# A hybrid decoder block: the second half's first norm moved from VectorE to ScalarE and GpSimd

## The reference

```python
def rmsnorm(x, g):
    xf = x.astype(jnp.float32)
    y = xf * lax.rsqrt(jnp.mean(xf * xf, axis=-1, keepdims=True) + EPS)
    return (y * g.astype(jnp.float32)).astype(x.dtype)
...
        h = rmsnorm(x, norm_mix[l])
        proj = jnp.einsum('bsd,de->bse', h, w_in[l])
        x_lru = proj[..., :D_LRU]
        g_lru = proj[..., D_LRU:2 * D_LRU]
        v_cm = proj[..., 2 * D_LRU:2 * D_LRU + D_CM]
        g_cm = proj[..., 2 * D_LRU + D_CM:]
        glu = v_cm * jax.nn.sigmoid(g_cm)
        d = causal_depthwise_conv(glu, dw31_w[l], dw31_b[l])
```

## Time and profile before

| | before |
|---|---|
| median of 3 runs (lowest, highest) | 2034.61 us (2033.06, 2035.32) |
| the profiled execution | 2033.8 us, span 2032.0 us |
| PE busy | 1945.1 us, 96% of the span |
| DVE busy | 1158.7 us, 57% |
| ACT busy | 785.1 us, 39% |
| POOL busy | 1064.7 us, 52% |

### The profile page before, as it was taken

How to read it: one execution, slowest core, us unless ns; L and a number is a source line. 1 busy time by engine, 2 the same in 40 slices (tenths; PEclk the granted TensorE clock), 3 DMA queues, 4 the chain that set the end, 5 groups by cost and what they waited for, 6 DMA issues and landing times.

```text
span 2032.0 us, 23427 instructions
## 1 busy us (share of the span) xinstructions
PE 1945.1 (96%) x8602; PEld 1601.1 (79%) x8602; DVE 1158.7 (57%) x1205; ACT 785.1 (39%) x896; POOL 1064.7 (52%) x384
## 2 busy tenths in 40 slices
PE   6999899978999799999999899999999999999998
PEld 5888687856887588888888688888888888888886
DVE  5899899988545544543344534334333544574546
ACT  6356756584544433333333433233232111321112
POOL 2477477864543557765555555555555335335431
PEclk9999999978999899999999999999999999999999
DMA  5223232244768323532325332232247322242312
GB/s 162 63 63 101 66 94 76 97 150 171 249 201 259 104 88 114 154 125 76 105 67 160 125 103 67 78 103 67 78 144 290 114 83 94 91 186 89 117 41 83
DMA packets 213392, 238.60 MB, mean 117 GB/s; under 512 B 9902, under 2 KB 165550, under 8 KB 210010
## 3 DMA queue, kind: packets, MB, share of 16 engines
q1 hardware_dynamic: 213338, 237.89, 35.6%
HBM read 172.84 MB, written 65.01 MB: 117 GB/s over the span
## 4 chain that ended last, share of the span: by engine, by line
PE 84%; DVE 5%; POOL 4%; issue 2%; DMA 2%; ACT 2%; SPq 1%; DVEq 0%; POOLq 0%; ACTq 0%
PE ps L1738 20%; PE ps L1739 20%; PE ps L1740 20%; PE acc L1738 8%; PE acc L1739 7%; PE acc L1740 7%; DVE acc L1554 1%; DMA y_raw<-d_scr 1%; DVE x L1716 1%; DVE x L1707 1%; PE ps L1763 1%; DVE wo_lo L1491 1%; DVE a_lo L1569 1%; POOL w_lo L690 1%; POOL a_lo L807 0%
## 5 line engine op out<-in xcount | busy, mean ns | idle before, releaser
L1554 DVE SCALAR_TENSOR_TENSOR acc<-glu,par,acc 128x1024 f32<-128x1024 f32 x232 | 299.0, 1289 | 7.2
L802 POOL TENSOR_TENSOR t_lo<-t_sum,t_hi 128x2048 fp32r<-128x2048 f32 x44 | 204.3, 4643 | 179.3 <-ACT t_hi L1194 179.3
L796 POOL TENSOR_TENSOR b_lo<-m_raw,b_hi 128x1536 fp32r<-128x1536 f32 x44 | 158.4, 3599 | 209.4 <-ACT b_hi L1189 209.4
L1593 DVE TENSOR_TENSOR t_sum<-m_raw 128x512 f32<-128x512 f32 x88 | 134.6, 1532 | 207.7 <-PE acc L1740 110.0
L1707 DVE TENSOR_TENSOR x<-x,ps 128x512 f32<-128x512 f32 x264 | 179.5, 688 | 108.5 <-PE ps L1740 108.5
L872 POOL TENSOR_TENSOR f_lo<-f_raw,f_hi 128x2048 fp32r<-128x2048 f32 x22 | 102.5, 4659 | 260.1 <-ACT f_hi L1332 260.1
L1738 PE MATMUL ps<-h_hi,w_hi 128*128 128x512 f32 x512 | 202.0, 395 | 5.1 <-POOL w_lo L690 2.6
L1738 PE MATMUL ps<-wd_hi,f_hi 128*128 128x512 f32 x528 | 205.5, 389 | 0.2 <-DVE x L1707 0.2
L1739 PE MATMUL ps<-wd_lo,f_hi 128*128 128x512 f32 x528 | 205.4, 389 | 0.0
L1740 PE MATMUL ps<-wd_hi,f_lo 128*128 128x512 f32 x528 | 205.4, 389 | 0.0
L1739 PE MATMUL ps<-h_lo,w_hi 128*128 128x512 f32 x512 | 199.9, 390 | 0.0
(11 more groups left out here) (208 smaller groups left out, 4539.7 us busy)
## 6 DMA issues: line engine op xcount, KB each, us to landing
m_raw<-in_w_gate SPq DMA_DIRECT2D x88, 256.0 KB, 4.1
m_raw<-in_w_up SPq DMA_DIRECT2D x88, 256.0 KB, 3.8
f_scr<-gt SPq DMA_DIRECT2D x88, 256.0 KB, 2.4
f_raw<-f_scr SPq DMA_DIRECT2D x22, 1024.0 KB, 4.8
wd_raw<-in_w_down SPq DMA_DIRECT2D x22, 1024.0 KB, 4.9
w_raw<-in_w_in SPq DMA_DIRECT2D x32, 512.0 KB, 5.3
xt<-in_x SPq DMA_DIRECT2D x16, 512.0 KB, 4.1
row<-in_x SPq DMA_DIRECT2D x16, 512.0 KB, 4.9
```

The lines of the kernel that those rows point to most:

```text
L796: g.tensor_tensor(b_lo[b][:, :, :, :], m_raw[b][:, 0:3], f32(b_hi[b][:, :, :, :]), ALU.subtract).then_inc(s_mlo, 1)
L802: g.tensor_tensor(t_lo[b][:, :, :, :], t_sum[b][:, :, :, :], f32(t_hi[b][:, :, :, :]), ALU.subtract).then_inc(s_mlo, 1)
L1554: ins = v.scalar_tensor_tensor(out=into[:, :], in0=t[:, k:k + HALF], scalar=col(j, R_DW + k), in1=acc[:, :], op0=ALU.mult, op1=ALU.add)
L1593: v.tensor_tensor(into, in0, in1, ALU.subtract).then_inc(s_t, 1)
```

## The change

In the first half nothing changes. For tiles 8 to 15, `x_norm` is split in three: VectorE keeps the reciprocal (`x_reciprocal`, each one tap earlier than `x_norm` was), ScalarE multiplies the tile by it (`x_scale`), and GpSimd multiplies by the weight row (`x_gain`). Each step waits for the one before it, over two new semaphores.

```diff
         X_NORM_AT = (7, 8, 9, 10, 12, 13, 14, 15)
+        X_NORM_BETWEEN = 5
+        X_NORM_AT = (6, 7, 8, 9, 11, 12, 13, 14)
         X_LO_AT = (9, 10, 11, 12, 14, 15, 16, 17)
...
+            def x_gain(g):
+
+                pool.wait_ge(s_xsc, g - TPH + 1)
+                t = xt[g % 3]
+                nc.gpsimd.tensor_tensor(t[:, :], t[:, :], g_row[:, :], ALU.mult).then_inc(s_xn, 1)
...
                 if u >= 1:
                     gated_input(u - 1)
                     decay(u - 1)
+                    if u == NJ - 1:
+                        for n in range(X_NORM_BETWEEN):
+                            x_gain(TPH + n)
                     decay_square(u - 1)
+                if u == NJ - 1:
+                    x_gain(TPH + X_NORM_BETWEEN)
                 short_sums(u)
+                if u == NJ - 1:
+                    for n in range(X_NORM_BETWEEN + 1, TPH):
+                        x_gain(TPH + n)
...
+            def x_scale(g):
+                act.wait_ge(s_xrec, g - TPH + 1)
+                a.activation(xt[g % 3][:, :], xt[g % 3][:, :], ACT.Copy, scale=rstd[:, g:g + 1]).then_inc(s_xsc, 1)
...
                 if u == NJ - 1:
-                    for g in range(TPH, TPH + 3):
-                        x_std(g)
+                    x_std(TPH)
+                    x_std(TPH + 1)
+                    x_scale(TPH)
+                    x_std(TPH + 2)
+                    x_scale(TPH + 1)
+                    x_scale(TPH + 2)
...
                     x_std(TPH + 3)
                     x_hi(TPH + 1)
+                    x_scale(TPH + 3)
                     x_std(TPH + 4)
                     x_hi(TPH + 2)
+                    x_scale(TPH + 4)
                     x_hi(TPH + 3)
                     x_std(TPH + 5)
+                    x_scale(TPH + 5)
...
                     x_hi(TPH + 4)
                     x_std(TPH + 6)
-                if u == NJ - 1:
+                    x_scale(TPH + 6)
                     x_hi(TPH + 5)
                     x_std(TPH + 7)
+                    x_scale(TPH + 7)
                     x_hi(TPH + 6)
...
+            def x_reciprocal(g):
+                dve.wait_ge(s_std, g + 1)
+                v.reciprocal(rstd[:, g:g + 1], rstd[:, g:g + 1]).then_inc(s_xrec, 1)
+
...
                             if place == X_NORM_AT[g]:
-                                x_norm(TPH + g)
+                                x_reciprocal(TPH + g)
```

More of the change, by code:

```diff
@@ L203, in hybrid_block @@
         s_xn = sem("x_normed")
+        s_xrec = sem("x_reciprocal_ready")
+        s_xsc = sem("x_scaled")
         s_hhi = sem("h_hi_ready")
```

## The result

The changed kernel takes 2047.81 us, the median of 4 runs (2046.53 to 2048.32), against 2034.96 us (4 runs, 2033.06 to 2036.68): +12.85 us, a ratio of 1.0062 with a 95% interval of 1.0047 to 1.0077. It is slower, by the size forecast.

The account below looks back on a forecast made before the run. TensorE, busy nearly throughout, is bound by its waits. Delays through the scales, gain and inversion reach turn 15 as +12.4 us, never given back: 2032.0 + 12.4 = 2044.4 span, 2047.0 on the median's footing; range 2044.1 to 2049.1, 70 in 100.

Parts of the forecast that it names:

- Turn 8: Tile 8's transposes on TensorE wait for scale and gain: 210.2 instead of 206.97, +3.2 us, 5.3 idle before.
- Turns 9 and 10: Next transposes on TensorE: 215.7 after a low clock, then 220.6 after the later load, Sqrt and `x_lo(9)`.
- Up to `two_minus`: ScalarE's list with six added scales: `two_minus` starts at 228.9 instead of 223.07, +5.8 us.
- GpSimd: Tile 13's gain stands ahead of the first short sum, adding 1.7 us net; `x_hi(12)` moves to 238.45, +7.3.
- The reciprocal of tile 14: On VectorE it waits until 242.2 for tile 14's Sqrt, with a tap and `x_lo(12)` queued behind it.
- Turn 13: Tile 13's transposes on TensorE wait 12 us for `x_lo(12)`: 244.4 instead of 232.51, +11.9 us.
- the inversion: On VectorE, tile 14's reciprocal ahead of `x_lo(12)` waits for a Sqrt behind `x_hi(12)`; costs 4.5 us alone.
- Turns 14 and 15: Last transposes on TensorE, after tile 15's reciprocal ahead of `x_lo(13)`: 250.45 and 254.25, +12.2 us, or 255.1.
- the first of the two ways: Tile 15's transposes on TensorE at +12.2 us; the second, a low clock lasting 5.2 us, gave +13.1; +12.4 taken.
- rival 1: At tile 13's transposes, the 4.26 us wait absorbs earlier delay: +4.5 to +8, 2039 to 2043 us; 15 in 100.
- that only the inversion is left: Same as rival 1: delay up to Turn 13 absorbed, 2039 to 2043 us; 15 in 100.
- That VectorE's relief pays: Rival for VectorE's second-half passes: 1.5 us of TensorE waits vanish, 2033.1 us, no slower; 4 in 100.
- That a late stage falls apart: Rival at projection 9: `scan_input` or weight split slips, some 4 us more, 2051 us; 11 in 100.

Follow-up runs that it names:

- experiment 1: Changed kernel with the reciprocals of tiles 14 and 15 one tap later, behind `x_lo(12)` and `x_lo(13)`: 2045.1 us, ratio 1.0036.
- experiment 3: Kernel before with `x_norm(14)` put ahead of `x_lo(12)`, a tap between, no work moved between engines: 2041.11 us, ratio 1.0024.
- experiment 4: Kernel before with `x_hi(12)` and tile 14's Square and Sqrt ahead of the second evacuation, `x_hi(13)` and tile 15's behind the second product: 2033.09 us, ratio 0.9982.
- experiment 5: experiment 4 with VectorE's passes moved, `x_lo` one place earlier from tile 12 on, `x_hi(14)` ahead of the GELU table load: 2035.8 us, ratio 1.0005.
- experiment 8: Changed kernel with tile 8 alone normalised by VectorE's pass as before: 2045.1 us, ratio 1.0049.
- experiment 2: experiment 1 plus `two_minus` moved ahead of the first evacuation and `decay_square` behind the third gain: 2041.68 us, ratio 1.0026.
- experiment 6: experiment 1 with the gain as a VectorE pass one tap later, GpSimd's list as before, scales still on ScalarE: 2044.56 us, ratio 1.0047.
- experiment 7: Kernel before with the pass split: VectorE scales, GpSimd multiplies by the row, ScalarE's list untouched, reciprocals 14 and 15 behind the splits: 2039.95 us, ratio 1.0021.
- experiment 9: experiment 2 with the order of experiment 4, tile 14's scale ahead of the second evacuation and its gain ahead of the short sums: 2044.7 us, ratio 1.0045.
- experiment 10: experiment 9 with the gain of tile 15 ahead of the third short sum on GpSimd: 2041.69 us, ratio 1.0033.

## Why the prediction was right

Times after are given on the clock of the trace before (0.95 us taken off).

- *Turn 8* was forecast at 210.2 and came at 210.29, with 5.44 us of idle time before it (5.3), and at the low clock behind it (1.94 us for the transposes, 1.06 before). *Turns 9 and 10*: 215.5 (216.44 in the changed kernel's trace) and 220.5, forecast 215.7 and 220.6.
- *Up to `two_minus`*: 228.5, forecast 228.9. A scale lasted 0.09 us more than its price. The row that I took has constants for scale and bias, and L1022, a Copy with a scale per row, took 1.14 already before. It cost nothing, since from its start to the next instruction's it is 1.05 us (228.41 to 229.47), as priced. The turns ahead came 0.1 to 0.3 us sooner than forecast.
- *GpSimd*: the first short sum at 234.4 (234.9), the third product at 236.8 (237.4), `x_hi(12)` at 237.8 (238.45). From `two_minus` to the third product it is 8.25 us, 8.5 forecast and 7.00 before: the gain added 1.25, a little less than the 1.5 to 1.7 of the prediction, since nothing stretched it or the short sum behind it: taps and gains ran side by side.
- *The reciprocal of tile 14*: 241.6 (242.2), VectorE idle for 12.95 us (13). *Turn 13*: 243.6 (244.4), 11.40 us idle before it. Experiment 1 measured the inversion at 4.37 us (forecast 4.5); experiment 3 shows that it costs about as much without the rest.
- *Turns 14 and 15*: 249.6 and 253.4, forecast 250.45 and 254.25 or later. The low clock did not outlast the twelve matmuls, so the first of the two ways held; I had added 0.2 for the second.
- *Given back later*: nothing. The product of unit 4 is 11.2 us late on that clock.

Every step was thus right within about 0.8 us and somewhat too dear; turn 15 moved by 11.4, not 12.4. The total of +12.85 came out so near to +12.4 because 1.5 us that do not come from this stage lay on top, and that is luck. The traces show where such time is made. A split on GpSimd (L796) that starts at 1021.62 us in the trace of before is 12.27 us late in the change, and the one at 1299.70 is 14.49 late (no time taken off here). Between them TensorE waits for `a_lo`, 3.67 us before and 3.66 after; the 10 us behind this wait, before and then in the change:

```profile
1140.60:1150.60 10.00, 9.98 (x37) 8.15 (x38) 3.31 (x3) 1.97 (x2) 3.30 (x1) 0.83 0.00 0
```

```profile
1153.70:1163.70 10.00, 9.93 (x31) 7.90 (x32) 1.94 (x4) 1.96 (x2) 2.36 (x1) 0.69 0.00 0
```

Their mean granted clock is 0.69 instead of 0.83, so a longer part of them was at the 1.2 GHz level, and 31 matmuls ran where there had been 37, 1.4 us by the 0.227 us of a matmul at full speed. Another such place follows a wait of 2.6 us for `w_lo`, at 353.54 before. The 10 us behind it, before and in experiment 1:

```profile
353.50:363.50 10.00, 9.96 (x44) 8.26 (x45) 9.68 (x8) 6.39 (x8) 9.92 (x7) 1.00 0.64 212
```

```profile
361.50:371.50 10.00, 9.91 (x37) 8.05 (x38) 9.68 (x8) 4.87 (x7) 9.92 (x8) 0.83 0.66 212
```

The kernel before, the change and experiments 4, 5 and 8 have a granted clock of 1.00 and 43 or 44 matmuls there; experiments 1, 2, 3, 6, 7, 9 and 10 have 0.83 and 37, 7 matmuls fewer or 1.6 us more behind a wait that is equally long in all of them (2.55 to 2.69 us). That is most of what several rows of the table have above turn 15 (0.2 to 2.7 us; two rows are 0.6 to 0.7 below). Why the same wait is followed by the low clock in one kernel and not in the other stays open. The table sets one trace beside a median, too, and the times of one kernel spread by several us.

Two slips of the prediction changed nothing. The short sum in the earlier trace rows did not begin as the stretched pass ended but 0.4 us before (227.37 against 225.54 + 2.23 = 227.77), and the middle of rival 1's 2039 to 2043 is 2041, not 2041.5.

The rivals: that only the inversion is left is refuted by experiment 1 (+9 in time without it). That VectorE's relief pays is refuted by the result, and by experiments 2, 9 and 10 for the other orders tried: the split still cost 5.6, 8.9 and 6.3 us. That a late stage falls apart (+4 more) did not occur; `scan_input` and the weight split came in time.

## What to carry to other kernels

Ask of an engine to be relieved not how busy it is but who waits for it at that place: about 9.6 us of passes were taken off VectorE's list, and its waits ahead of the reciprocals grew from 3.9 to 24.3 us. On engines that work through a list in order, the place of a small instruction with a late wait decides: a reciprocal of 0.16 us one place too early cost 4.4 us, a gain behind a late sum 4.7 us of waiting; so for each instruction moved, write down what it waits for and what stands behind it. And where the idle time of the bound engine hangs on one chain, reorder that chain first: moving `x_hi(12)` and no work at all gave 3 us, more than any split.

## What the hardware showed that I had not expected

A VectorE pass that reads two SBUF tiles and a GpSimd product do not share the time, they take turns. In experiment 4 the pass ended 1.1 us after GpSimd's product both times (227.61 behind 226.53, 233.44 behind 232.35), however long it had been under way, and so did the passes that began during a product in the kernel before and in experiments 3 and 5: nearly its whole 1.28 us lies behind the product, and the cost is about what is left of the product when the pass begins, less 0.2, at most 2.1 us here. The reverse holds too: the short sum that began 1.0 us before such a pass ended took 3.22 us instead of 2.41. The plain tensor_scalar of experiment 7 behaves alike: 0.75 us alone, 1.68 beside a gain, ended 0.55 us behind it. Taps and `x_lo`, which read one operand from PSUM, ran at 1.28 beside gains of 2.35 to 2.40. The Trainium skill's page "GPSIMD Engine Reference", section 8, names this contention (VectorE instructions with two SBUF inputs or in a two-port mode) without a size. These runs agree and give the size; the 2.23 us in the earlier trace rows were the mild case of a pass that began with 1.14 us of the product left.
